# The first norm of a 17-stage transformer kernel: x turned by products with a diagonal of the roots, the gains applied in the copies out of PSUM

## The chip, the cores and the metric

The kernel runs on one core of one Trainium2 chip. The metric is the device time of one execution in microseconds; lower is better.

## The reference

Two transformer blocks follow one another on x of 256 tokens by 1024 channels, all in fp32. What matters here is the first thing that they do: a root-mean-square norm with gains, and the product with the first weight matrix.

```python
def rms_norm(x, g):          # x * rsqrt(mean(x*x) + eps) * g
...
def first_block(x, norm1_g, w_in, ...):
    for l in range(DEPTH):
        h = rms_norm(x, norm1_g[l])
        proj = h @ w_in[l]
        q, k, v, u = jnp.split(proj, [ATTN_WIDTH, 2 * ATTN_WIDTH, 3 * ATTN_WIDTH], axis=-1)
        ...   # attention over q, k, v; a gated causal convolution over u
        x = x + jnp.concatenate([attn, conv], axis=-1) @ w_out[l]
        h = rms_norm(x, norm2_g[l])
        x = x + (jax.nn.silu(h @ w_gate[l]) * (h @ w_up[l])) @ w_down[l]
    return x
```

Everything later (a feed-forward part, four more of them, two more mixers) is untouched by the change.

## The kernel before

Tokens lie in two tiles of 128 (t = 0, 1), channels in eight slices of 128 (k = 0 to 7, KT = 8). Weights come in units of 1 MB (`UNIT`): for the first mixer 1024 rows by 256 columns of `w_in`. Each fp32 operand is split in two fp32r parts, high and low. For weights ScalarE writes the high part `w_hi` (`split_hi`, L474) and VectorE the low one `w_lo` = raw - high (`split_lo`, L1892); for the turned activations the parts are `t_hi` and `t_lo`. A product is then three passes on TensorE: high by high, high by low, low by high. There are three raw buffers (`RAWS`) and six split slots. SyncE issues the loads in order, and the load of unit n waits for `lo_done` of unit n-3 (L424, L425): a raw buffer is free once VectorE has made the low part.

The engines' programs are written out by hand, one order for each engine, and tied by semaphores. The phases are an edge (norm and turning), a mixer, an edge, a feed-forward part and so on. The first edge, with `take == "input"`, goes so:

- SyncE loads the two tiles of x, then unit 0 in two halves (L435, L436), then units 1 and 2. ScalarE's queue loads the gains as one line (`g_line`, L954) and the identity (L955).
- TensorE spreads the gains over 128 partitions: two fp32 products of a column of ones with the line, 512 columns each, into banks 0 and 1 (L1315). `keep_running(3, 1)` (L1339) is one product of a constant with itself; its result is not used.
- ScalarE squares and sums the first half of each tile (`edge_stats`, L493) as soon as the tile is in, VectorE the other half (`mean_square`, L1987), and VectorE adds both and eps (L1990). GpSimd raises this to the power -0.5 (`inv_root`, L981): the root, one number for each token, one instruction for each tile. Behind these two, GpSimd's queue has six small setup loads (L986 to L991).
- VectorE makes `xn` = gains * root * x in four pieces (`normed`, L1995), TensorE turns each by transposes with the identity (L1323, four for each piece, sixteen in all), ScalarE and VectorE copy the turned pieces out of PSUM as `t_hi` (L551, L2018), VectorE subtracts for `t_lo` (`turned`, L2004). Between these lie the halves of unit 0's high part (L484, L489) and low part (L2023, L2034).
- Unit 0 (`by_channels_first`, L1147) is 48 passes of 256 columns in two halves of k; each half is high by high, high by low, then low weights by high. Unit 1 (`by_channels_second`, L1169 to L1174) runs 16 passes before it first waits for the low parts of its own weights; the units after it go by `three` (L1120 to L1122).

Behind unit 0, TensorE turns some parameters (`turn_params`, L1334), ScalarE copies them (L565, L566). Then the first mixer runs: VectorE, ScalarE and GpSimd share the 31 taps of the convolution (L2203 and L2206; L711 and L715; L1040 and L1043), and GpSimd builds diagonal matrices of taps for TensorE (L1055) once VectorE has done `setup` (L2563, L2571). TensorE's next products wait in its own order behind these.

Of the kernel before, what the change touches and what calls it, by code (L numbers as in the profile page):

```python
# [63 lines left out]
def build(nc, a, out, phases):  # L64
    stack = ExitStack()
    with stack:
# [43 lines left out]
        xn = wv(0, T, D)  # L110
        junk = wv(5120, 2, D)
# [130 lines left out]
        second_hi = sem("second_hi")  # L242
        line_in = sem("line_in")
        ones_set = sem("ones_set")
        g_spread = sem("g_spread")
# [88 lines left out]
        for ph in phases:  # L334
# [25 lines left out]
            n_lo += {"edge": 2 * T * (ph.get("g") is not None), "ffn": 0, "mix": 4}[ph["kind"]]  # L360
# [38 lines left out]
        index_bank = (4, 5, 2, 3)  # L399

# [57 lines left out]
        def _(act):  # L458
# [87 lines left out]
            def input_turned(t, half):  # L546

                nx(x_T)
                act.wait_ge(x_T, 2 * half + t + 1)
                src = bank[phases[0]["xb"][t] + half].rearrange("p (k s) -> p k s", k=4)  # L550
                nc.scalar.activation(t_hi[:, 4 * half:4 * half + 4, t * P:(t + 1) * P], src, ACT.Copy).then_inc(t_hi_ok, 1)  # L551

            def edge(ph):
                if ph["take"] == "input":
                    edge_stats(ph, 0)
                    edge_stats(ph, 1)
                    input_turned(0, 0)
                    first_half()
                    nx(x_T)
                    input_turned(0, 1)  # L560
                    input_turned(1, 1)
# [405 lines left out]
        def _(pool):  # L967
# [30 lines left out]
            def next_rows(post):  # L998

                if post and n_post < len(posts):  # L1000
                    pool.wait_ge(yg_done, 2 * T * n_post)
                    pool.dma_start(g_row[:, :], posts[n_post]["row"].partition_broadcast(P)).then_inc(grow_in, 16)
                if n_pre < len(pres):
                    pool.wait_ge(xn_ready, 2 * T * (n_pre + 1))
                    pool.dma_start(g_pre[:, :], pres[n_pre]["g"].partition_broadcast(P)).then_inc(gpre_in, 16)
# [105 lines left out]
        def _(pe):  # L1111
# [28 lines left out]
            def by_channels_first(b):  # L1140

                wh, wl = w_cols(0)
                def part(half, w, x, start=False, stop=False):

                    for c in range(2):
                        for k in range(4 * half, 4 * half + 4):
                            mm = nc.tensor.matmul(bank[b][:, c * S:(c + 1) * S], w[:, k, c * P:(c + 1) * P], x[:, k, :],  # L1147
                                                  start=start and k == 0 and c == 0, stop=stop and k == KT - 1 and c == 1)
                    return mm

                for half in range(2):
                    pe.wait_ge(hi_done if half else half_hi, 1)
                    pe.wait_ge(t_hi_ok, 2 * half + 1)
                    pe.wait_ge(second_hi, 1)
                    part(half, wh, t_hi, start=half == 0)
                    pe.wait_ge(t_lo_ok, 2 * half + 2)
                    part(half, wh, t_lo)
                    pe.wait_ge(lo_done if half else half_lo, 1)
                    mm = part(half, wl, t_hi, stop=half == 1)
# [17 lines left out]
            def tile_ready(t, k):  # L1177

                if k % 4 == 0:
# [128 lines left out]
            def edge(ph):  # L1308
                if ph["g"] is None:
                    return  # L1310
                if ph["take"] == "input":
                    pe.wait_ge(ones_set, 1)
                    pe.wait_ge(line_in, 16)
                    for h in range(2):
                        nc.tensor.matmul(bank[h][:, :], ones, g_line[:, h * 512:(h + 1) * 512], start=True, stop=True).then_inc(g_spread, 1)  # L1315
                    pe.wait_ge(consts_set, 2)
                    keep_running(3, 1)
                    pe.wait_ge(ident_in, 16)
                    for half in range(2):
                        for t in range(T):  # L1320
                            pe.wait_ge(xn_ready, nx(xn_ready))
                            for k in range(4 * half, 4 * half + 4):
                                mm = nc.tensor.transpose(bank[ph["xb"][t] + half][:, k % 4 * P:(k % 4 + 1) * P],  # L1323
                                                         xn[:, t, k * P:(k + 1) * P], ident[:, :])
                            mm.then_inc(x_T, 1)
# [541 lines left out]
        def _(dve):  # L1867
# [113 lines left out]
            def input_edge(ph):  # L1981
# [11 lines left out]
                def normed(t, h):  # L1993
                    hv = slice(h * 512, (h + 1) * 512)
                    nc.vector.scalar_tensor_tensor(out=xn[:, t, hv], in0=bank[h][:, :], scalar=st[:, 2 + t:3 + t],  # L1995
                                                   in1=x_sb[:, t, hv], op0=ALU.mult, op1=ALU.mult).then_inc(xn_ready, 1)

                def turned(t, half):
                    if (t, half) == (1, 0):
                        dve.wait_ge(second_hi, 1)  # L2000
                    else:
                        dve.wait_ge(t_hi_ok, (1, 2 + t)[half])
                    ks, ts = slice(4 * half, 4 * half + 4), slice(t * P, (t + 1) * P)
                    nc.vector.tensor_tensor(t_lo[:, ks, ts], bank[ph["xb"][t] + half].rearrange("p (k s) -> p k s", k=4),  # L2004
                                            t_hi[:, ks, ts].bitcast(F32), ALU.subtract).then_inc(t_lo_ok, 1)
# [3 lines left out]
                dve.wait_ge(g_spread, 1)  # L2009
                dve.wait_ge(rstd_ready, nx(rstd_ready))  # L2010
# [621 lines left out]
```

## Time and profile before

| | us |
|---|---|
| median of 3 runs | 1287.6 |
| lowest, highest | 1285.88, 1287.77 |
| the profiled execution, its own time | 1287.3 |
| its span, first to last instruction | 1285.4 |
| outside the span | 1.9 |
| TensorE busy in the span | 1274.2 (99%) |
| weight loads busy | 1088.2 (85%) |
| VectorE busy | 838.1 (65%) |
| ScalarE busy | 676.7 (53%) |
| GpSimd busy | 120.1 (9%) |

Busy means that an instruction of the engine was under way; matmuls overlap each other, so the steady pace of an engine is read from how far apart their starts are, not from their durations. Times of rows are microseconds from the first instruction. A "PEld" row is a weight load, which every matmul has. An fp32 product shows as two matmuls, a transpose or an fp32r product as one.

### The profile page before, as it was taken

What the parts mean: (1) busy time and instruction counts of PE and PEld (TensorE: products, weight loads), DVE (VectorE), ACT (ScalarE), POOL (GpSimd) and SP (SyncE); (2) the same over time, 40 slices, a digit from 0 to 9 for tenths busy, and PEclk for the clock granted to TensorE, in tenths of its full rate; (3) what the DMA queues carried; (4) which work ended last, traced back from release to release, by engine and by line L of the source; (5) the groups of instructions that cost most, each with busy time, mean ns of one, the idle gap of its engine ahead of it and who ended that gap; (6) DMA issues with size and microseconds to landing.
All of it is one profiled execution on the core that took longest, in us unless ns stands there. A gap on an engine that the chain in (4) does not pass through costs nothing.

```text
span 1285.4 us, 18283 instructions
## 1 busy us (share of the span) xinstructions
PE 1274.2 (99%) x7072; PEld 1088.2 (85%) x7072; DVE 838.1 (65%) x1102; ACT 676.7 (53%) x903; POOL 120.1 (9%) x135
## 2 busy tenths in 40 slices
PE   8999999999999999999999999999999999999998
PEld 7978888888888888887888888888888877888886
DVE  7997655565655548898765556655565776675552
ACT  5876554443544435656564444544454665564441
POOL 4970000000000000021000000000002120000000
PEclk9999999999999999999999999999999999999999
DMA  9525765563765543527565555575553755475540
GB/s 278 175 83 192 253 210 196 196 210 120 241 201 188 188 150 122 174 88 241 197 223 185 183 194 163 199 260 196 190 186 128 245 160 165 148 239 185 184 145 33
DMA packets 174350, 234.95 MB, mean 183 GB/s; under 512 B 4351, under 2 KB 154127, under 8 KB 174288
## 3 DMA queue, kind: packets, MB, share of 16 engines
q1 hardware_dynamic: 170368, 223.52, 52.9%
q0 software_dynamic: 3184, 9.37, 2.4%
q10 hardware_dynamic: 736, 1.19, 0.3%
q8 instruction: 43, 0.70, 0.2%
q14 instruction: 19, 0.16, 0.0%
HBM read 233.03 MB, written 1.05 MB: 182 GB/s over the span
## 4 chain that ended last, share of the span: by engine, by line
PE 90%; POOL 3%; DVE 3%; ACT 1%; DMA 1%; issue 1%; DVEq 0%; SPq 0%; POOLq 0%; ACTq 0%
PE psum L1225 23%; PE psum L1120 14%; PE psum L1121 14%; PE psum L1122 14%; PE psum L1233 12%; PE psum L1246 2%; POOL ws L1043 2%; PE psum L1188 2%; PE psum L1187 2%; PE psum L1186 2%; PE psum L1250 1%; PE psum L1457 1%; PE psum L1348 1%; POOL ws L1040 1%; PE psum L1505 1%
## 5 line engine op out<-in xcount | busy, mean ns | idle before, releaser
L1892 DVE TENSOR_TENSOR w_lo<-raw,w_hi 128x2048 fp32r<-128x2048 f32 (+1 forms) x200 | 457.7, 2294 | 85.2 <-ACT w_hi L474 83.8
L474 ACT ACTIVATE w_hi<-raw 128x2048 fp32r<-128x2048 f32 (+1 forms) x212 | 403.4, 1907 | 34.5 <-PE psum L1122 13.7
L1225 PE MATMUL psum<-t_both,w_hi 128*128 128x512 f32 x1280 | 304.7, 390 | 0.0
L1225 PEld LDWEIGHTS psum<-t_both,w_hi 128*128 128x128 f32 x1280 | 237.4, 188 | 47.4
L1120 PE MATMUL psum<-w_hi,f_hi 128*128 128x512 f32 x488 | 192.8, 395 | 0.0
L1122 PE MATMUL psum<-w_hi,f_lo 128*128 128x512 f32 x488 | 190.2, 390 | 0.0
L1121 PE MATMUL psum<-w_lo,f_hi 128*128 128x512 f32 x488 | 190.1, 389 | 0.0
L1120 PE MATMUL psum<-w_hi,t_both 128*128 128x512 f32 (+2 forms) x464 | 166.0, 358 | 0.2
L1122 PE MATMUL psum<-w_hi,t_both 128*128 128x512 f32 (+2 forms) x464 | 162.3, 350 | 0.0
L1121 PE MATMUL psum<-w_lo,t_both 128*128 128x512 f32 (+2 forms) x464 | 162.3, 350 | 0.0
L1233 PEld LDWEIGHTS psum<-t_both,w_lo 128*128 128x128 f32 x1280 | 158.9, 192 | 3.1
L1233 PE MATMUL psum<-t_both,w_lo 128*128 128x256 f32 x1280 | 159.8, 283 | 0.0
L589 ACT ACTIVATE ws<-psum 128x512 f32<-128x512 f32 x40 | 23.9, 597 | 256.1 <-PE psum L1233 256.1
L2064 DVE TENSOR_TENSOR ws<-psum,ws 128x512 f32<-128x512 f32 x40 | 27.6, 690 | 196.3 <-ACT ws L589 196.3
L981 POOL TENSOR_TENSOR st<-st,minus_half 128x1 f32<-128x1 f32 (+3 forms) x35 | 31.2, 891 | 1084.3 <-DVE st L1939 764.7
L1122 PEld LDWEIGHTS psum<-w_hi,f_lo 128*128 128x128 f32 x488 | 91.6, 188 | 19.3
L1120 PEld LDWEIGHTS psum<-w_hi,f_hi 128*128 128x128 f32 x488 | 91.6, 188 | 18.6 <-issue 0.5
L1121 PEld LDWEIGHTS psum<-w_lo,f_hi 128*128 128x128 f32 x488 | 91.7, 188 | 18.1
L1120 PEld LDWEIGHTS psum<-w_hi,t_both 128*128 128x128 f32 x464 | 87.7, 189 | 15.5 <-issue 3.7
L1122 PEld LDWEIGHTS psum<-w_hi,t_both 128*128 128x128 f32 x464 | 87.6, 189 | 11.7
L1121 PEld LDWEIGHTS psum<-w_lo,t_both 128*128 128x128 f32 x464 | 87.8, 189 | 10.3
L685 ACT ACTIVATE ws<-ws,st 128x128 f32<-128x128 f32 x80 | 35.4, 445 | 18.8 <-DVE st L2167 18.8
(218 smaller groups left out, 1291.1 us busy)
## 6 DMA issues: line engine op xcount, KB each, us to landing
raw<-in_ffn_wg SPq DMA_DIRECT2D x44, 1024.0 KB, 5.6
raw<-in_ffn_wu SPq DMA_DIRECT2D x44, 1024.0 KB, 5.4
raw<-in_ffn_wd SPq DMA_DIRECT2D x44, 1024.0 KB, 5.0
raw<-in_even_w_in SPq DMA_DIRECT2D x12, 1024.0 KB, 5.3
raw<-in_odd_w_in SPq DMA_DIRECT2D x12, 1024.0 KB, 5.3
raw<-in_w_gate SPq DMA_DIRECT2D x11, 1024.0 KB, 5.6
raw<-in_w_up SPq DMA_DIRECT2D x11, 1024.0 KB, 5.4
raw<-in_w_down SPq DMA_DIRECT2D x11, 1024.0 KB, 5.1
```

The lines of the kernel that those rows point to most:

```text
L474: nc.scalar.activation(w_hi[:, n % SLOTS, 0:w], raw[:, n % RAWS, 0:w], ACT.Copy).then_inc(hi_done, 1)
L685: nc.scalar.activation(p_buf[:, h % 2, lo:hi], s_buf[:, h % 2, lo:hi], ACT.Exp, scale=-1.0, bias=L["nmax"][:, c:c + 1], accum_out=L["sum"] ...
L981: nc.gpsimd.tensor_tensor(v, v, minus_half[:, 0:1].broadcast_to([P, v.shape[1]]), ALU.pow).then_inc(rstd_ready, 1)
L1043: nc.gpsimd.tensor_tensor(acc[:, 1::2, :], acc[:, 1::2, :], product[:, tap % 2, :, :], ALU.add)\
L1120: nc.tensor.matmul(o, lh, rh, start=start, stop=False)
L1121: nc.tensor.matmul(o, lh, rl, start=False, stop=False)
L1122: return nc.tensor.matmul(o, ll, rh, start=False, stop=stop)
L1186: nc.tensor.matmul(out, t_hi[:, k, ts], wh(k), start=k == 0, stop=False)
L1225: mm = nc.tensor.matmul(bank[b + c][:, :], wh[:, k, c * P:(c + 1) * P], t_both[:, k, :, :].rearrange("p a s -> p (a s)"), start=k == 0 and ...
L1233: mm = nc.tensor.matmul(bank[b + c][:, 0:S], wl[:, k, c * P:(c + 1) * P], t_hi[:, k, :], start=k == 0 and low_first, stop=k == KT - 1 and ...
L1892: nc.vector.tensor_tensor(w_lo[:, n % SLOTS, 0:w], raw[:, n % RAWS, 0:w], w_hi[:, n % SLOTS, 0:w].bitcast(F32), ALU.subtract).then_inc(lo_ ...
L2064: nc.vector.tensor_tensor(halves(f_s[:, b, :]), halves_of(4)[0], f_b[:, 0, :, :], ALU.add).then_inc(gate_sum, 1)
```

## The change

1. **TensorE first.** `keep_running(3, 28)` comes first, where it was `keep_running(3, 1)` behind the spread. The spread of the gains is gone. In its place eight products of a 1x128 piece of the line with one one put the gains as a column for each slice k into bank 2 (`gains_T` is raised behind the last).
2. **ScalarE first.** Its first compute instruction is now the copy of these eight columns to `gain_col`, which waits for `gains_T`. `edge_stats` for both tiles stands behind it. Then it writes `root_at_diag[0]`, the identity scaled by tile 0's roots; VectorE writes the one of tile 1.
3. **Turning.** `normed` and the transposes are gone. TensorE multiplies each 128x128 block of x, as weights, with the diagonal matrix of its tile: eight fp32 products for each tile, into `first_T(k)`, where slice k has both tiles side by side (256 columns).
4. **Copies.** `t_hi` for k = 0, 1 is made by VectorE, for 2 to 7 by ScalarE, one instruction of 256 columns for each k with the gain as its scale. `t_lo` is (PSUM * gain) - `t_hi` on VectorE, eight instructions of 256 columns.
5. **Orders.** Unit 0's passes go k by k: high weights by `t_hi` for k 0 to 3, low weights by `t_hi` for 0 to 3, high weights by `t_lo` for 0 to 3, then the same for 4 to 7. ScalarE makes the first half of `w_hi` before its `t_hi` and the second half behind them. Waits on counts are adapted (`tile_ready`, GpSimd's `next_rows`).

```diff
@@ ScalarE
             def edge(ph):
                 if ph["take"] == "input":
+                    act.wait_ge(gains_T, 1)
+                    nc.scalar.activation(gain_col, bank[2][:, 0:KT], ACT.Copy).then_inc(gains_kept, 1)
                     edge_stats(ph, 0)
                     edge_stats(ph, 1)
-                    input_turned(0, 0)
+                    act.wait_ge(ident_in, 16)
+                    act.wait_ge(rstd_ready, 1)
+                    nc.scalar.activation(root_at_diag[0], ident[:, :], ACT.Copy, scale=st[:, 2:3]).then_inc(root_diag, 1)
                     first_half()
-                    nx(x_T)
-                    input_turned(0, 1)
-                    input_turned(1, 1)
+                    act.wait_ge(gains_kept, 1)
+                    for k in range(2, KT):
+                        first_hi(k)
                     second_half()
@@ TensorE, edge
+                    pe.wait_ge(consts_set, 2)
+                    keep_running(3, 28)
                     pe.wait_ge(ones_set, 1)
                     pe.wait_ge(line_in, 16)
-                    for h in range(2):
-                        nc.tensor.matmul(bank[h][:, :], ones, g_line[:, h * 512:(h + 1) * 512], start=True, stop=True).then_inc(g_spread, 1)
-                    pe.wait_ge(consts_set, 2)
-                    keep_running(3, 1)
...
+                    for k in range(KT):
+                        mm = nc.tensor.matmul(bank[2][:, k:k + 1], g_line[:, k * P:(k + 1) * P], ones[:, 0:1], start=True, stop=True)
+                    mm.then_inc(gains_T, 1)
+                    for t in range(T):
+                        pe.wait_ge(root_diag, t + 1)
+                        for k in range(KT):
+                            nc.tensor.matmul(first_T(k)[:, t * P:(t + 1) * P], x_sb[:, t, k * P:(k + 1) * P], root_at_diag[t],
+                                             start=True, stop=True).then_inc(x_scaled, 1)
@@ TensorE, unit 0
+                pe.wait_ge(half_hi, 1)
+                for k in (0, 1):
+                    pe.wait_ge(dve_hi, k + 1)
+                    high(k, t_hi, start=k == 0)
+                for k in (2, 3):
+                    pe.wait_ge(act_hi, k - 1)
+                    high(k, t_hi)
+                pe.wait_ge(half_lo, 1)
+                low(0)
+                for k in range(4):
+                    pe.wait_ge(first_lo, k + 1)
+                    high(k, t_lo)
...
@@ VectorE, input_edge
                 mean_square(0)
                 mean_square(1)
-                dve.wait_ge(g_spread, 1)
-                dve.wait_ge(rstd_ready, nx(rstd_ready))
-                normed(0, 0)
...
+                dve.wait_ge(ident_in, 16)
+                dve.wait_ge(rstd_ready, nx(rstd_ready, 2))
+                dve.wait_ge(root_diag, 1)
+                nc.vector.tensor_scalar(root_at_diag[1], ident[:, :], st[:, 3:4], None, ALU.mult).then_inc(root_diag, 1)
+                dve.wait_ge(gains_kept, 1)
+                dve.wait_ge(x_scaled, KT + 2)
+                for k in range(2):
+                    nc.vector.tensor_scalar(t_hi[:, k, :], first_T(k), gain_col[:, k:k + 1], None, ALU.mult).then_inc(dve_hi, 1)
                 dve.wait_ge(half_hi, 1)
                 h = slice(0, UNIT // 2)
                 nc.vector.tensor_tensor(w_lo[:, 0, h], raw[:, 0, h], w_hi[:, 0, h].bitcast(F32), ALU.subtract).then_inc(half_lo, 1)
...
+                for k in range(4):
+                    low(k)
+                dve.wait_ge(half_lo, 1)
+                dve.wait_ge(hi_done, 1)
+                h = slice(UNIT // 2, UNIT)
+                nc.vector.tensor_tensor(w_lo[:, 0, h], raw[:, 0, h], w_hi[:, 0, h].bitcast(F32), ALU.subtract).then_inc(lo_done, 1)
+                for k in range(4, KT):
+                    low(k)
```

## Rows read from the trace of the kernel before

**Rows 1.** The page's busy shares; tenths in 40 slices.

```profile
PE 1274.2 (99%) x7072; PEld 1088.2 (85%) x7072; DVE 838.1 (65%) x1102; ACT 676.7 (53%) x903; POOL 120.1 (9%) x135
PE   8999999999999999999999999999999999999998
```

**Rows 2.** Waits of weight loads, 17 us to the end: total, times, longest.

```profile
PEld psum L1505 <- issue: 5.6, 15, 0.9
PEld psum L1457 <- issue: 5.3, 19, 0.4
...
PEld psum L1470 <- POOL ws L1012: 0.9, 2, 0.6
```

**Rows 3.** Timeline of TensorE to 19.5 us: start, us, what, count.

```profile
3.30 3.75 PE L1315 MATMUL psum<-ws 1*128 1x512 f32 x4 [3.30 <-DMA ws<-in_norm_g]
6.98 0.79 PE L1339 MATMUL psum<-mean_w 128*128 128x128 f32 x2
8.03 3.65 PE L1323 MATMUL psum<-ident,ws 128*128 128x128 f32 x16 [0.26 <-DVE ws L1995]
11.32 2.28 PE L1147 MATMUL psum<-t_both,w_hi 128*128 128x256 f32 x16
...
16.32 1.12 PE L1147 MATMUL psum<-t_both,w_lo 128*128 128x256 f32 x8
17.37 0.49 PE L1334 MATMUL psum<-ident,ws 20*128 20x20 f32 x2
```

**Rows 4.** Timeline, the other engines, 0.7 to 8 us.

```profile
0.78 0.21 POOL L975 MEMSET mean_w<- 128x128 f32 x1
4.65 0.63 ACT L493 ACTIVATE ws<-x_sb 128x512 f32<-128x512 f32 x1 [0.90 <-DMA x_sb<-in_x]
5.50 0.21 DVE L1990 TENSOR_SCALAR st<-st 128x1 f32<-128x1 f32 x1
5.86 0.55 POOL L981 TENSOR_TENSOR st<-st,minus_half 128x1 f32<-128x1 f32 x1 [4.87 <-DVE st L1990]
6.18 0.69 DVE L1987 CUSTOM_DVE_ANT_0 ws<-x_sb 128x512 f32<-128x512 f32 x1 [0.47 <-DMA x_sb<-in_x]
7.30 0.56 POOL L981 TENSOR_TENSOR st<-st,minus_half 128x1 f32<-128x1 f32 x1 [0.89 <-DVE st L1990]
```

**Rows 5.** Timeline, fp32 products later in the kernel, near 100 us.

```profile
99.25 1.86 PEld L1838 LDWEIGHTS psum<-mean_w,g_row 128*128 128x128 f32 x16 [0.64 <-ACT g_row L791]
102.53 0.61 PE L1844 MATMUL psum<-ident,st 128*128 128x128 f32 x4
```

**Rows 6.** Windows at the end: busy (count) by engine, PEclk, DMA, GB/s.

```profile
1270.00:1279.30 9.30, 9.30 (x43) 7.36 (x41) 2.82 (x5) 1.46 (x4) 0.56 (x1) 1.00 0.15 58
1279.40:1281.30 1.90, 0.00 (x0) 0.00 (x0) 1.12 (x4) 0.67 (x2) 0.55 (x1) 1.00 0.00 0
1281.40:1285.40 4.00, 0.00 (x0) 0.00 (x0) 1.04 (x2) 0.00 (x0) 0.00 (x0) 0.50 0.35 131
```

**Rows 7.** Timeline of ScalarE and VectorE, 10 to 18 us.

```profile
9.64 1.05 ACT L484 ACTIVATE w_hi<-raw 128x1024 fp32r<-128x1024 f32 x1
10.61 1.28 DVE L2004 TENSOR_TENSOR t_both<-psum,t_both 128x512 fp32r<-128x512 f32 x2
11.80 1.21 DVE L2023 TENSOR_TENSOR w_lo<-raw,w_hi 128x1024 fp32r<-128x1024 f32 x1
14.14 1.21 DVE L2034 TENSOR_TENSOR w_lo<-raw,w_hi 128x1024 fp32r<-128x1024 f32 x1
15.27 2.28 DVE L1892 TENSOR_TENSOR w_lo<-raw,w_hi 128x2048 fp32r<-128x2048 f32 x1
17.89 0.19 ACT L565 ACTIVATE p_col<-psum 128x20 f32<-128x20 f32 x1 [2.84 <-PE psum L1334]
17.98 0.27 ACT L566 ACTIVATE tap_col<-psum 128x124 f32<-128x124 f32 x1
```

**Rows 8.** Timeline, 256-column instructions out of PSUM, ScalarE and VectorE.

```profile
21.51 0.84 ACT L698 ACTIVATE ws<-psum,p_col 128x256 f32<-128x256 f32 x2
23.85 0.88 DVE L2220 SCALAR_TENSOR_TENSOR ws<-psum,p_col,ws 128x256 f32<-128x256 f32 x2 [0.99 <-PE psum L1174]
```

**Rows 9.** The chain that ended last, 17 to 30 us: start, us, what.

```profile
17.58 9.67 DMA raw<-in_w_in
27.27 1.92 ACT w_hi L474
29.66 2.70 POOL ws L1040
```

More of the change, by code:

```diff
@@ L241, in build @@
         half_lo = sem("half_lo")
[L242 removed]
+        gains_T = sem("gains_T")
+        gains_kept = sem("gains_kept")
+        root_diag = sem("root_diag")
+        x_scaled = sem("x_scaled")
+        dve_hi = sem("dve_hi")
+        act_hi = sem("act_hi")
+        first_lo = sem("first_lo")
         line_in = sem("line_in")
         ones_set = sem("ones_set")
[L245 removed]
         setup_in = [sem(f"setup_in{i}") for i in range(3)]
@@ L359, in build @@
                 n_x += 2 * T
-            n_lo += {"edge": 2 * T * (ph.get("g") is not None), "ffn": 0, "mix": 4}[ph["kind"]]
+            n_lo += {"edge": 2 * T * (ph.get("g") is not None and ph.get("take") != "input"), "ffn": 0, "mix": 4}[ph["kind"]]
             n_rstd += {"edge": T * (ph.get("take") == "post") + T * (ph.get("g") is not None), "ffn": 0,
@@ L1142, in by_channels_first, with high @@
                 wh, wl = w_cols(0)
-                def part(half, w, x, start=False, stop=False):
+                def high(k, x, start=False, stop=False):
                     for c in range(2):
-                        for k in range(4 * half, 4 * half + 4):
-                            mm = nc.tensor.matmul(bank[b][:, c * S:(c + 1) * S], w[:, k, c * P:(c + 1) * P], x[:, k, :],
-                                                  start=start and k == 0 and c == 0, stop=stop and k == KT - 1 and c == 1)
-                    return mm
@@ L1151, in by_channels_first @@
[L1151 to L1159, printed above, removed]
+                        mm = nc.tensor.matmul(bank[b][:, c * S:(c + 1) * S], wh[:, k, c * P:(c + 1) * P], x[:, k, :],
+                                              start=start and c == 0, stop=stop and c == 1)
@@ new lines, in high, with low @@
+                    return mm
+                def low(half):
+                    for k in range(4 * half, 4 * half + 4):
+                        for c in range(2):
+                            nc.tensor.matmul(bank[b][:, c * S:(c + 1) * S], wl[:, k, c * P:(c + 1) * P], t_hi[:, k, :], start=False, stop=False)
+                pe.wait_ge(half_hi, 1)
[5 more added lines that the diff above has]
+                    high(k, t_hi)
@@ new lines, in by_channels_first @@
+                pe.wait_ge(half_lo, 1)
[3 more added lines that the diff above has]
+                    high(k, t_lo)
+                pe.wait_ge(hi_done, 1)
+                for k in range(4, KT):
+                    pe.wait_ge(act_hi, k - 1)
+                    high(k, t_hi)
+                pe.wait_ge(lo_done, 1)
+                low(1)
+                for k in range(4, KT):
+                    pe.wait_ge(first_lo, k + 1)
+                    mm = high(k, t_lo, stop=k == KT - 1)
@@ L1177, in tile_ready @@
             def tile_ready(t, k):
-                if k % 4 == 0:
+                if k % 4 == 0 and fresh[0] is not None:
                     pe.wait_ge(t_lo_ok, fresh[0] + 2 * t + k // 4 + 1)
@@ L1991, in mean_square, with low @@
                                             ALU.add, ALU.add).then_inc(ms_ready, 1)
[L1993 to L2005, printed above, removed]
+                def low(k):
+                    if k >= 2:
+                        dve.wait_ge(act_hi, k // 2 * 2)
+                    nc.vector.scalar_tensor_tensor(out=t_lo[:, k, :], in0=first_T(k), scalar=gain_col[:, k:k + 1], in1=t_hi[:, k, :].bitcast(F32),
+                                                   op0=ALU.mult, op1=ALU.subtract).then_inc(first_lo, 1)
@@ L2030, in edge @@
                     input_edge(ph)
-                    dve.wait_ge(half_lo, 1)
-                    dve.wait_ge(hi_done, 1)
-                    h = slice(UNIT // 2, UNIT)
-                    nc.vector.tensor_tensor(w_lo[:, 0, h], raw[:, 0, h], w_hi[:, 0, h].bitcast(F32), ALU.subtract).then_inc(lo_done, 1)
                     cur[0] = 1
```

39 lines of the change are left out of this document (13 added, 26 removed).

## The prediction

> **What bounds the kernel now.** I read the page first. TensorE is busy for 99% of the span and in every one of the 40 slices [rows 1]. A busy share alone doesn't make it the bound, so I asked next what its weight loads waited for once unit 0 was over. From 17 us to the end the longest single wait is 0.9 us, and the largest group on another engine's work adds up to 0.9 us [rows 2]; the rest is the fixed half microsecond at the head of small groups. So from the first product of unit 0 on TensorE runs nearly without a gap, and whatever moves the end of unit 0 moves the end of the kernel by nearly the same. Next comes the timeline of the start, where the change lies: TensorE's first products start at 3.30, the sixteen transposes at 8.03, unit 0 at 11.32, and unit 0 ends at 17.4 [rows 3]. The question of this prediction is therefore one number: when does unit 0 end now?
>
> Two paces are to be seen there. The sixteen transposes fill 3.65 us, and the last one's own latency is 0.42 of it, so their starts are 0.213 us apart; sixteen passes of 256 columns behind them fill 2.28 us, about 0.12 to 0.13 apart [rows 3]. Later in the kernel four fp32 matmuls of 128 columns fill 0.61 us with 0.27 for one, and sixteen loads of one-column products fill 1.86 with 0.19 for one: 0.11 us apart in both [rows 5]. So the array is at 1.2 GHz until about 11.3 and at 2.4 GHz behind that. It rises after 3.3 to 3.6 us in which the transposes ran without a gap. It did not rise for the 3.75 us of one-row products before them. A fall shows too, at the end of the kernel: 1.9 us without products are still granted 1.00, the next 4 us 0.50 [rows 6].
>
> **The change part by part.** I build the new start forward, TensorE first.
>
> Step 1, `keep_running(3, 28)`. One product is two matmuls [rows 3], so 28 are 56. Their constant is set at 1.0 [rows 4] and nothing else is waited for, so they start at 1.1. At the low pace 0.213 they last 11.9 us, at the high one 0.11 they last 6.2: the end lies between 7.3 and 13.0. I take a rise at 4.7, after the same uninterrupted run as in the trace: 17 matmuls until then, 39 at 0.11 behind, the end at 9.0. These matmuls do nothing else, so in front of anything they hold back they cost their full time.
>
> Step 2, the gains. Eight fp32 products are 16 matmuls with a 128-column weight load each; by the one-column group 0.11 each [rows 5], 1.8 us (3.4 at the low pace). `gains_T` comes with 0.25 latency at about 11.1.
>
> Step 3, what waits for it. ScalarE's first instruction now waits for `gains_T`, and behind it stand both `edge_stats`. This is the place that decides. The copy is 0.2 us [rows 7], so the squares of tile 0 start at T0 = 11.3 instead of 4.65 [rows 4], although x has been there for 6.6 us. VectorE's sum, GpSimd's root and everything else wait behind it. From T0: the root of tile 0 is there at +1.8 (6.41 less 4.65), ScalarE's diagonal matrix (0.27, as the 124-column copy [rows 7]) at +2.1. VectorE can start the squares of tile 1 only at about +1.1; its part of them, sum, root (0.56) and the matrix give +3.1.
>
> Step 4, x times the diagonal. Sixteen fp32 products are 32 matmuls where sixteen transposes were 16. At 0.11 they last 3.5 us, at 0.213 6.8. They start at T0 + 2.1 = 13.4. TensorE has then had nothing at all for 2.5 us, and only one-row, one-column work for 1.8 us ahead of that; the trace shows a fall within about 2 us of the last product [rows 6], and that one-row work did not hold or lift the clock [rows 3]. So I take 1.2 GHz again at 13.4, and a rise after the same run as before, 3.6 us: 17 matmuls, then 15 at 0.11. The end is 13.4 + 3.6 + 1.65 = 18.6. Without the fall it is 16.9; without a rise 20.2.
>
> The Trainium skill (TensorE: Matmul & The Clock Gate, Part 4) says that transposes don't count as activity for the clock the way products do. The trace agrees that all sixteen ran at the low pace, but the first products behind them were fast at once, so here the measurement decides. Under the page's rule the rise in the old kernel would be put down to the products before the transposes, and my rise in step 1 could be later by as much as the bounds of that step hold.
>
> The same page (Part 3, the cost of the semaphore tail) prices each product that raises a semaphore at 26 ns, and `x_scaled` is raised by all sixteen. By it the sum would be 0.4 us larger. No row here isolates it.
>
> Step 5, unit 0. Its 48 passes at 0.12 are 5.8 us, unchanged. VectorE's share begins when slices 0 and 1 of tile 1 are in PSUM, 20 of the 32 matmuls in, at 17.5. It has two scalings, the half of `w_lo`, four low parts, the other half and four more: ten PSUM instructions of 256 columns at 0.33 (half of the 512-column pitch, 0.60 [rows 7]) to 0.44 [rows 8], two halves at 1.13: 5.6 to 6.7, and it ends at 23.1 to 24.2. ScalarE has six `t_hi` at about 0.38 [rows 8], the last one when the products are over, then the second half (1.05), by about 20. Its first half lies under the products. TensorE, from 18.6, ends at 24.4, with VectorE's last low parts just ahead of it. That is 7.0 us behind 17.4.
>
> What is removed and comes back: four `normed` (2.8 us on VectorE) and the transposes. They lay ahead of unit 0 and their removal is in the sum already, as the new chain doesn't hold them.
>
> Step 6, what is late next. VectorE's low part of unit 1 starts 7 to 8 us later, about 23.5, and takes 2.3 [rows 7]: TensorE can do unit 1's first 16 passes (1.9 us) from 24.9 meanwhile, so it doesn't stop. The loads of units 3 and 4 go out with `lo_done` of 0 and 1. In the old kernel the load of unit 4 took 9.67 us [rows 9] because it ran beside unit 3's load and the six loads of GpSimd's queue. Those loads are issued after the roots, now at about 14.2, with raw buffers full and nothing beside them, and are in before unit 3's load goes out; nearer 5 to 6 us for a load gives ScalarE's split of unit 4 about 4 us late, not 7. GpSimd's taps hang on that (29.66 [rows 9]) and are late by less than TensorE. So the convolution chain is no new bound; the few waits on other engines shrink, for which I give back 0.6 us.
>
> The unlisted edits (`tile_ready`, `next_rows`, ten small waits) cost nothing: TensorE's waits there are met by work that ended earlier, and GpSimd's first g_pre load already has its own place. Uncovered they'd be an instruction of some 0.05 us each.
>
> Sum: +7.0 - 0.6 = +6.4 us. The profiled execution took 1287.3 (span 1285.4 and 1.9 around it), 0.3 under the median of the three runs; 1287.3 + 6.4 = 1293.7, and with the 0.3, 1294.0.
>
> **Rivals.** (a) The clock doesn't fall in the gap: a gap of 2.5 us is hardly longer than the 1.9 that was still granted 1.00 [rows 6]. Then the products with the diagonals end at 16.9, unit 0 at 22.8, and the time is +4.8: 1292.4. Against it stand 1.8 us of nearly idle work on top.
> (b) The rise comes much later, or `keep_running` stays at the low pace. Each microsecond of delay of the rise in step 1 costs 0.5 us; for all 56 slow and slow gains the end of unit 0 goes from 24.4 to about 30, +11.5: 1299. For it speaks that the rise before came 4.3 us after the first full product at 6.98, or 8 us after the first of all [rows 3]; this last reading would give T0 = 13.5 and 1296.3.
> (c) The other side: faster. If the 56 matmuls and the gains were over when x is in, at 4.65, the statistics would be as early as before, the diagonal matrices there at 7.2 and 8.2, the products done by 10.8 and unit 0 by 16.6: 0.8 us less, 1286.8, which is no change by measure. For more, the low pace would have to be lifted too. It would decide if a matmul of `keep_running` took under 0.03 us ((4.4 - 1.1 - 1.8)/56); the fastest row has 0.11. It is as good as excluded by that place.
> (d) The delay is absorbed later. It would take a stretch in which TensorE waits for loads or for another engine by several microseconds; the waits [rows 2] don't have one, and all but the 0.6 given back would be a surprise. If half of it is lost the time is 1290.8; if all but 2 us, 1289.3.
>
> **How the numbers follow.** Forecast (fall, rise as before) 0.50, (a) 0.25, (b) 0.13, (c) 0.04, (d) 0.08. The predicted time is that of the first, 1294.0. Between 1290.2 and 1298 lie the forecast, (a), most of (b) and the milder (d): more than 8 in 10. A difference of 0.2% or 2.6 us is about what a measurement of this kernel can tell from no change. Slower than that: the first three and half of (d), 0.91; no change: half of (d) and most of (c), 0.07; faster 0.02.
>
> **What the new profile would show.** Step 1: 56 matmuls of `mean_w` from 1.1 to about 9, their starts 0.213 apart, then 0.11. Step 3: ScalarE's first squares at about 11.3, with TensorE as the releaser of the copy before them. Step 4: a gap of some 2.5 us on TensorE ahead of the products with `x_sb`, then 0.213 again. Step 5: unit 0's last pass at about 24.4. Step 6: from there on the two timelines run parallel, 6 to 7 us apart to the end. The prediction is wrong if the squares start before 9, if the pace of `keep_running` is below 0.11, or if the distance between the two kernels' TensorE shrinks by more than 1.5 us behind unit 0.

## The result, and the profile after

The changed kernel takes 1295.35 us (median of six runs, 1294.27 to 1296.02); the kernel before took 1286.8 in its six runs beside them (1285.88 to 1287.77). These medians are 8.55 us apart, or 0.66%; the ratio estimated from the runs is a little lower, 1.0057, with a 95% interval of 1.0048 to 1.0067. Either is well over the 0.2% that can be told from no change. Forecast were 1294.0, with 1290.2 to 1298.0. The profiled execution took 1295.7, its span is 1293.9 against 1285.4: +8.5, where the forecast had +6.4.

The time is lost in the first 26 us. TensorE's timeline of the start, which answers to [rows 3]:

```profile
1.04 8.61 PE L1370 MATMUL psum<-mean_w 128*128 128x128 f32 x56 [1.04 <-POOL mean_w L987]
9.58 1.94 PE L1347 MATMUL psum<-ws 1*128 1x1 f32 x16
14.24 6.15 PE L1352 MATMUL psum<-ws,x_sb 128*128 128x128 f32 x32 [2.71 <-ACT ws L569]
20.14 1.20 PE L1159 MATMUL psum<-t_both,w_hi 128*128 128x256 f32 x8
21.18 1.12 PE L1167 MATMUL psum<-t_both,w_lo 128*128 128x256 f32 x8
...
26.33 0.49 PE L1365 MATMUL psum<-ident,ws 20*128 20x20 f32 x2
```

`turn_params`, the first work behind unit 0, starts at 26.33, where it started at 17.37 [rows 3]. I use the start of this row as the mark for the end of unit 0 in every kernel below. Here it is 9.0 later than before. (The last experiment profiles the start of the old kernel a second time, and there the mark stood at 18.1. So differences of some tenths between marks mean little.) The order of events is the forecast's: 56 matmuls of a constant, 16 one-row matmuls for the gains, a gap of 2.71 in which TensorE waits for ScalarE's diagonal matrix (L569), and 32 matmuls with x.

What ScalarE and the other engines did meanwhile (their timelines, compare [rows 4]):

```profile
4.61 0.69 DVE L2018 CUSTOM_DVE_ANT_0 ws<-x_sb 128x512 f32<-128x512 f32 x1 [3.61 <-DMA x_sb<-in_x]
11.56 0.18 ACT L564 ACTIVATE ws<-psum 128x8 f32<-128x8 f32 x1 [7.80 <-PE psum L1347]
11.63 0.62 ACT L503 ACTIVATE ws<-x_sb 128x512 f32<-128x512 f32 x1
12.47 0.21 DVE L2021 TENSOR_SCALAR st<-st 128x1 f32<-128x1 f32 x1 [7.15 <-ACT ws L503]
12.83 1.38 POOL L993 TENSOR_TENSOR st<-st,minus_half 128x1 f32<-128x1 f32 x2 [11.84 <-DVE st L2021]
13.79 0.40 ACT L569 ACTIVATE ws<-ident,st 128x128 f32<-128x128 f32 x1 [0.83 <-POOL st L993]
18.98 0.88 DVE L2040 TENSOR_SCALAR t_both<-psum,ws 128x256 fp32r<-128x256 f32 x2 [4.38 <-PE psum L1352]
```

VectorE squares its half of tile 0 at 4.61, since x is there. ScalarE's half starts at 11.63, right behind the copy of the gains, and the copy had been waiting 7.80 us for TensorE. VectorE then waits 7.15 for that half, GpSimd 11.84. The chain that ended last runs through exactly these instructions, with no transfer in this part of it:

```profile
1.04 8.61 PE psum L1370 x56
9.65 1.89 PE psum L1347 x16
11.56 0.18 ACT ws L564
11.74 0.62 ACT ws L503 x2
12.47 0.22 DVE st L2021
12.83 0.86 POOL st L993
13.79 0.41 ACT ws L569
14.24 6.15 PE psum L1352 x32
```

The windows show the clock (busy and count by engine, then the granted clock, DMA share, GB/s):

```profile
5.50:12.20 6.70, 6.03 (x53) 5.82 (x52) 0.00 (x0) 0.64 (x3) 0.00 (x0) 1.00 1.10 350
12.30:19.10 6.80, 4.86 (x23) 4.86 (x24) 1.44 (x6) 2.00 (x5) 4.89 (x8) 0.50 0.73 182
19.20:25.00 5.80, 5.80 (x49) 5.60 (x48) 5.42 (x11) 5.04 (x8) 0.00 (x0) 1.00 0.13 47
```

It is at 1.00 (2.4 GHz) from 5.5, falls to 0.50 (1.2 GHz) at 12.3, in the gap behind the one-row matmuls, and stays there for the first 23 matmuls with x, whose starts are 0.213 apart; the nine behind them are at the high pace, 0.112 to 0.128 apart. Ahead of the first rise the profile has no record of the clock and a window reads 1.00 whatever the pace; there I go by how far apart the starts are.

### The profile page after: what moved, and what is told of

It is laid out like the page before. It is cut to its first block, busy times and chain, and to the rows that moved or that the text cites. A ratio compares the mean times of both kernels' runs of the same rounds, so it can differ in the third digit from the quotient of the medians.

```text
span 1293.9 us, 18450 instructions
## 1 busy us (share of the span) xinstructions
PE 1282.8 (99%) x7154; PEld 1099.4 (85%) x7154; DVE 836.3 (65%) x1104; ACT 677.0 (52%) x908; POOL 119.2 (9%) x135
## 4 chain that ended last, share of the span: by engine, by line
PE 96%; DVE 2%; ACT 1%; POOL 1%; issue 0%; DVEq 0%; ACTq 0%; POOLq 0%
PE psum L1255 23%; PE psum L1133 15%; PE psum L1134 15%; PE psum L1135 15%; PE psum L1263 12%; PE psum L1276 2%; PE psum L1218 2%; PE psum L1217 2%; PE psum L1216 2%; PE psum L1488 1%; PE psum L1280 1%; PE psum L1379 1%; PE psum L1536 1%; PE psum L1501 1%; PE psum L1370 1%; DVE w_lo L1923 1%
## 5 line engine op out<-in xcount | busy, mean ns | idle before, releaser
L1134 PEld LDWEIGHTS psum<-w_lo,f_hi 128*128 128x128 f32 x488 | 91.7, 188 | 18.1
```

The lines of the kernel that those rows point to most:

```text
L1134: nc.tensor.matmul(o, lh, rl, start=False, stop=False)
```

## The experiments

Theory: the change loses its time because ScalarE's statistics stand behind `gains_T`, and so behind `keep_running(3, 28)` and the gains; to this comes the low clock in the products with x. Rivals: the new way of turning x is itself the dearer one; or the constant products pay for themselves with the clock; or what is late in the first 26 us is made up for, or added to, later. For each run I give median and range, the ratio to the kernel before in the same job with its 95% interval, the mark of the profiled execution, and the span less the mark, which is all that comes behind unit 0 (1268.0 in the kernel before, 1267.6 in the changed one).

**Statistics first.** ScalarE's wait and copy are moved behind the statistics and the diagonal matrix; TensorE's program is untouched.

```diff
 if ph["take"] == "input":
-    act.wait_ge(gains_T, 1)
-    nc.scalar.activation(gain_col, bank[2][:, 0:KT], ACT.Copy).then_inc(gains_kept, 1)
     edge_stats(ph, 0)
     ...
     nc.scalar.activation(root_at_diag[0], ...).then_inc(root_diag, 1)
+    act.wait_ge(gains_T, 1)
+    nc.scalar.activation(gain_col, bank[2][:, 0:KT], ACT.Copy).then_inc(gains_kept, 1)
```

> The changed kernel with one edit: ScalarE's copy of the gain columns, and its wait for them, stand behind the squares of both tiles and the diagonal matrix of tile 0; TensorE still starts with 28 products. Theory A (the time is lost because the statistics wait for the gains, and these for the 28 products): the squares start at 4.65 again, the diagonal matrix of tile 0 is there at 7.3 and waits for TensorE, which goes from the gains (end 11.4) straight into the products with x, at the high pace (0.11): these end near 15.1, unit 0 near 21.2, 5 us ahead of the changed kernel: 1290.2 to 1290.8. Theory B (the doubled matmuls for x and the 256-column copies cost the time, whatever the order): within 1.5 us of the changed kernel's 1295.35.

Measured: 1291.67 (1291.41 to 1292.12), 1.0031 [1.0018, 1.0044], mark 21.90, behind it 1268.2. Its timeline:

```profile
6.65 0.39 ACT L567 ACTIVATE ws<-ident,st 128x128 f32<-128x128 f32 x1
...
1.04 9.27 PE L1370 MATMUL psum<-mean_w 128*128 128x128 f32 x56 [1.04 <-POOL mean_w L987]
10.24 1.94 PE L1347 MATMUL psum<-ws 1*128 1x1 f32 x16
12.11 3.84 PE L1352 MATMUL psum<-ws,x_sb 128*128 128x128 f32 x32
```

The diagonal matrix is there at 7.0 instead of 14.2, the gap on TensorE is gone, and with it the low clock: 3.84 for the products with x instead of 6.15. Unit 0 ends 4.4 earlier, 2.1 by the earlier start (although the constant's matmuls took 0.66 longer in this profile) and 2.3 by the clock. Of the 9.0 us 4.5 are left: the constant's matmuls and the gains' hold up x now, where they held up ScalarE. It came 1 us above what was expected: about 0.7 at the mark, from the constant's matmuls, and 0.6 behind unit 0 (below).

**The number of constant products.** One instead of 28, and 56, all else as in the change.

```diff
-    keep_running(3, 28)
+    keep_running(3, 1)      # the other run: keep_running(3, 56)
```

> The changed kernel with keep_running(3, 1) in place of 28. Theory A: the gains' line comes at 3.3, the gains take 16 matmuls at the low pace (3.4 us), so ScalarE starts its squares at 6.9 and not 11.6; the products with x start at 9.5, all or nearly all of them at the low pace (6.2 to 6.8 us), unit 0 ends near 22: 1291.0, 4.3 us less than the changed kernel. A rival (the 28 products are worth their time because without them the clock stays low for longer): the low pace reaches into unit 0, whose 48 passes then take up to 6 us more, and the time is 1295 or above.

> The changed kernel with keep_running(3, 56). Theory A: 56 more matmuls at 0.112 hold back the gains, the statistics and all behind them by 6.25 us one to one, give or take the phase in which the clock rises in the products with x: 1300.2 to 1302. Theory B (the 28 products lie beside the loading of x and the weights): under 1 us more, 1296.3 at most.

Measured: with one, 1289.66 (1289.10 to 1290.67), 1.0017 [1.0008, 1.0026], mark 20.13, behind it 1267.2. With 56, 1302.13 (1301.8 to 1302.33), 1.0112 [1.0097, 1.0128], mark 32.96, behind it 1267.1. TensorE with one:

```profile
2.31 3.54 PE L1347 MATMUL psum<-ws 1*128 1x1 f32 x16 [0.47 <-DMA ws<-in_norm_g]
8.56 5.62 PE L1352 MATMUL psum<-ws,x_sb 128*128 128x128 f32 x32 [2.72 <-ACT ws L569]
20.13 0.49 PE L1365 MATMUL psum<-ident,ws 20*128 20x20 f32 x2
```

and with 56:

```profile
1.04 15.01 PE L1370 MATMUL psum<-mean_w 128*128 128x128 f32 x112 [1.04 <-POOL mean_w L987]
20.64 6.50 PE L1352 MATMUL psum<-ws,x_sb 128*128 128x128 f32 x32 [2.71 <-ACT ws L569]
```

From 28 to 56 the span grows by 6.2, 56 times 0.112: each constant matmul stands on the path at its full time. (The mark moves by 6.6: two more of the products with x are at the low pace.) From 28 to one the span falls by 6.6. What the 27 products buy is a faster pace for the gains, 1.94 us instead of 3.54, and nothing for x, which begins at the low pace in every one of the three. So the rival that they pay for themselves is out. With one product the time is 1.3 us lower than expected, since the gains' line comes 1 us earlier than I had it and the low pace lasts for fewer of the products with x; with 56 it lies 0.1 above the range. The gap of 2.7 is the same in all three kernels: it is the length of the chain from `gains_T` to the diagonal matrix.

**The gap filled.** Twelve more constant products behind the gains, while TensorE waits for the diagonal matrix anyway.

```diff
     mm.then_inc(gains_T, 1)
+    keep_running(3, 12)
```

> The changed kernel with 12 more products of the constant behind the gains, where TensorE stood idle from 11.5 to 14.2 (24 matmuls at 0.112, 2.7 us). If the fall of the clock costs what the sum says: no fall at 12.3, the 32 matmuls with x 0.112 apart from the first on, 3.6 us instead of 5.9, and VectorE gets its first slices at 16.7 instead of 19.0: 2.3 us less, 1293.0. If the clock falls all the same (the one-row products count for nothing), or if VectorE's chain sets the end of unit 0 anyway, less than 0.5 us is gained.

Measured: 1293.82 (1293.61 to 1294.26), 1.0048 [1.0035, 1.0062], mark 23.30, behind it 1268.5. Timeline and windows:

```profile
8.86 1.94 PE L1347 MATMUL psum<-ws 1*128 1x1 f32 x16
10.73 2.94 PE L1371 MATMUL psum<-mean_w 128*128 128x128 f32 x24
13.52 3.84 PE L1353 MATMUL psum<-ws,x_sb 128*128 128x128 f32 x32
```

```profile
4.00:17.00 13.00, 13.00 (x115) 12.83 (x115) 2.89 (x10) 3.18 (x9) 4.88 (x8) 1.00 0.97 307
```

The clock holds. The mark is 3.03 earlier than in the changed kernel: 2.31 by x at the high pace, 0.72 because the rise came earlier in this profile (at 3.9). So the low clock by itself costs 2.3 us of the 9.0, as expected. In the medians only 1.5 us is to be seen: in the profile of this kernel 0.9 us more passes behind unit 0, where the clock falls once near 106 us (below).

**Statistics first, and fewer constant products.** Both edits together, with 17 and with one.

> The order of the first experiment (statistics ahead of the gains' copy) with keep_running(3, 17). In all five kernels so far the span is 1267.1 to 1268.4 us plus the end of unit 0. TensorE is through with the 34 matmuls near 7 and with the gains near 9, 2 us behind the diagonal matrix of tile 0 (7.3); the products with x run at the high pace to 12.5, unit 0 ends near 18.7. Theory A: 1287.9 to 1288.9, 1.2 us over the kernel before and 3 under the order alone. If it is 1290 or more, something else than TensorE's work ahead of x counts.

> The same order with keep_running(3, 1). The gains end at 5.9, the squares start at 4.6, the diagonal matrix is there at 7.3 and TensorE waits for it. The products with x start at 7.3 at the low pace; where the clock rises decides: at best 11.5 (20 slow matmuls, the rest 1.3 us), end 12.9, unit 0 near 19.1; at worst all 32 slow, end 14.1, unit 0 near 20.3. 1288.1 to 1289.5. Against the kernel before it shows what the new way of turning x costs by itself when neither the 28 products nor the order of ScalarE hold it up: 1.5 to 3 us. If the new way is better by itself, it is under 1287.

Measured: with 17, 1288.40 (1287.33 to 1290.17), 1.0009 [1.0000, 1.0018], mark 20.74, behind it 1267.5. With one, 1288.12 (1287.72 to 1288.83), 1.0006 [0.9997, 1.0015], mark 18.20, behind it 1268.7. With one the time lies at the lower end of its range and can't be told from the kernel before. The cost of the new way by itself, which I had put at 1.5 to 3 us, comes out at 0.3 in the medians and 0.8 at the mark. With 17 the median is in the range, but the mark is 2 us late, and the eleven runs lie in two groups, 1287.33 to 1288.40 and 1289.96 to 1290.17. The profiled execution is of the slower group (1290.01). Its timeline and two windows show why it is late:

```profile
7.46 1.94 PE L1347 MATMUL psum<-ws 1*128 1x1 f32 x16
9.33 5.47 PE L1352 MATMUL psum<-ws,x_sb 128*128 128x128 f32 x32
```

```profile
6.20:9.50 3.30, 3.30 (x29) 3.16 (x29) 1.00 (x4) 1.94 (x5) 0.60 (x2) 1.00 1.11 344
9.60:12.90 3.30, 3.30 (x17) 3.30 (x17) 0.00 (x0) 0.01 (x1) 2.88 (x5) 0.50 1.10 348
```

There is no gap, and still the clock falls, in the products with x just behind the one-row ones. With 28 products and the same order (the first experiment) the same sixteen one-row products, without a gap as well, were followed by x at the high pace. So to close the gap is enough in some executions and not in others. That the faster group of this kernel is the one without the fall fits the 2 us between the groups, but no execution of it was profiled.

**Gains loaded as columns.** What is left of the change when no product is spent on the gains at all: a transfer brings them in as columns, and 18 constant products lie where TensorE waits for the roots anyway.

```diff
-act.dma_start(g_line, phases[0]["g"].unsqueeze(0)).then_inc(line_in, 16)
+act.dma_start(gain_col, phases[0]["g"].rearrange("(k p) -> p k", p=P)).then_inc(line_in, 16)   # behind the identity's load
...
-keep_running(3, 28)
-... (eight products into bank[2], gains_T, the copy to gain_col)
+keep_running(3, 18)
```

> The best that I see in the new way: the gains come as columns by a load of their own (1024 pieces of 4 bytes, behind the identity's load in the same queue) instead of 16 matmuls and a copy, and keep_running(3, 18) ends near 7.1, when the diagonal matrix is ready. Products with x from 7.3 to 10.9 at the high pace, VectorE's first slices at 9.7, unit 0 near 16.9: 0.5 us ahead of the kernel before, 1286.9 to 1287.5 against its 1287.8. If the small pieces arrive later than 9.7, or delay x and the weights, it is slower than before by as much.

Measured: 1287.18 (1286.24 to 1287.98), 0.9997 [0.9988, 1.0006], mark 17.13, behind it 1268.9.

```profile
1.04 5.88 PE L1363 MATMUL psum<-mean_w 128*128 128x128 f32 x36 [1.04 <-POOL mean_w L985]
7.36 3.84 PE L1345 MATMUL psum<-ws,x_sb 128*128 128x128 f32 x32 [0.44 <-ACT ws L567]
17.13 0.49 PE L1358 MATMUL psum<-ident,ws 20*128 20x20 f32 x2
```

The mark is 0.24 before that of the old kernel. The old start alone was 0.7 apart in its two profiles, so this is no gain. Turning x by products with a diagonal, with the gains in the copies, comes to the same time as `normed` and transposes, once nothing stands ahead of the statistics, the gains cost TensorE nothing and the clock is up when x comes. Against this kernel the changed one is 9.20 late at the mark, and its 9.20 are 6.88 by which the products with x start late (14.24 less 7.36) and 2.31 by which they last longer.

**The old kernel with the clock lifted early.** Ten constant products ahead of the spread of the gains, three behind it.

> The kernel before with keep_running(3, 10) ahead of the spread of the gains and (3, 3) behind it in place of (3, 1), nothing else. If the clock rises by 6 or so and stays, the sixteen transposes are 0.11 apart instead of 0.213, but VectorE hands over its four pieces at 7.9, 8.6, 9.3 and 10.0, so they end at 10.5 instead of 11.3, and unit 0 starts when VectorE's copy of tile 1 is done (10.7): 0.5 us gained, unit 0 ends at 16.9, no difference that the time can show. Rival: the spread comes later (7.1 instead of 7.0 at best; later still at the low pace), VectorE's first piece with it, and nothing is gained.

Measured: 1287.47 (1286.07 to 1289.24), 0.9998 [0.9989, 1.0007], mark 17.25, behind it 1268.9. A miss in its mechanism: the mark should have come at 16.9.

```profile
5.16 1.98 PE L1317 MATMUL psum<-ws 1*128 1x512 f32 x4
7.98 3.60 PE L1325 MATMUL psum<-ident,ws 128*128 128x128 f32 x16
```

```profile
4.70:8.00 3.30, 3.30 (x16) 1.79 (x14) 2.58 (x8) 1.38 (x4) 1.10 (x2) 1.00 1.07 365
8.10:11.40 3.30, 3.30 (x17) 3.28 (x17) 3.29 (x6) 2.14 (x3) 1.23 (x2) 0.50 1.11 342
```

The one-row spread ran at 1.00. Behind it came the six matmuls of the constant, still at the high pace, and at 8.0, as the transposes began, the clock fell.

**The other order of passes.** The kernel with loaded columns, but unit 0's passes as before the change (in each half, low weights last).

> The kernel with the gains loaded as columns, and in unit 0 the old order of passes in each half: low parts of x before low parts of the weights. VectorE makes t_lo one slice in 0.39 us, TensorE uses one in 0.24, so in this order it waits for t_lo where it did the low weights before. Worked out from the trace of the kernel with the loaded columns: unit 0 ends at 17.7 instead of 17.05, 0.65 us later, which is what the new order of passes is worth here; in the time it is hardly to be told. If the end is at 17.1 or less, the new order is worth nothing.

Measured: 1287.22 (1286.82 to 1288.94), 0.9999 [0.9990, 1.0008], mark 18.05, behind it 1269.1. The mark is 0.92 later than in the kernel with the new order: TensorE waits for VectorE's low parts of x ahead of L1157. So the new order is worth 0.7 to 0.9 us to the new way of turning (0.65 expected), less than can be told in the median.

```profile
11.03 1.19 PE L1157 MATMUL psum<-t_both,w_hi 128*128 128x256 f32 x8
12.50 1.68 PE L1157 MATMUL psum<-t_both,w_hi 128*128 128x256 f32 x8 [0.28 <-DVE t_both L2023]
```

**What comes behind unit 0.** Span less mark is 1267.1 to 1268.0 in some kernels and 1268.2 to 1269.1 in the others. In the second kind, and only there, the clock is at 0.50 for a stretch between 100 and 110 us, behind a stretch of short waits and one-column products for a variance. This happens in some executions of a kernel and not in others. Of the kernel with the old order of passes, six runs took 1286.82 to 1287.22 with a mean granted clock of 0.999 or 1.000, and five 1288.46 to 1288.94 with 0.997 or 0.998; the profiled one is of the five and has the fall. The profile of the kernel with loaded columns is of this kind too:

```profile
98.05 1.95 PE L1862 MATMUL psum<-mean_w,g_row 128*128 128x1 f32 x16 [0.20 <-ACT g_row L801]
...
96.00:100.00 4.00, 3.81 (x26) 3.12 (x25) 3.15 (x3) 3.97 (x5) 0.00 (x0) 1.00 0.00 0
100.00:103.40 3.40, 3.40 (x11) 2.82 (x12) 0.16 (x1) 1.31 (x1) 1.27 (x2) 0.50 0.88 270
```

To see whether these products are the cause, I let them move 128 columns of the constant instead of one, in the kernel with loaded columns and in the old one.

```diff
-mm = nc.tensor.matmul(bank[4][:, S + t:S + t + 1], V["sq"][:, ct, t * P:(t + 1) * P], mean_w[:, 0:1], ...
+mm = nc.tensor.matmul(bank[4][:, S + t * P:S + (t + 1) * P], V["sq"][:, ct, t * P:(t + 1) * P], mean_w[:, :], ...
-nc.vector.tensor_scalar(st[:, 10:12], bank[4][:, S:S + T], ...
+nc.vector.tensor_scalar(st[:, 10:12], bank[4][:, S:2 * S:P], ...
```

> The kernel with the gains loaded as columns, plus one edit near 98 us: the sixteen matmuls of the variance move 128 columns of the constant instead of one (they were 0.11 apart with one column and should stay so with 128), so that the waits and one-column products there are no longer one quiet stretch. In the profile without this edit unit 0 ended 0.4 us ahead of the kernel before, but the granted clock fell to 0.50 from 100 to 103.4, in four other kernels of this study too, and the span was 0.6 us longer. If that fall is the cause: granted clock 1.00 from 100 to 110, the span 1267.1 to 1267.8 plus the end of unit 0, 1284.3 to 1284.9, and a median 0.5 to 1.3 us under the kernel before. If the fall costs nothing, the median is as without the edit, 0.3 to 0.6 under.

> The kernel before with the wide variance alone. Where the clock falls near 100 depends on when the clock's grants change in that execution, so some executions of the kernel before should have the fall and some not. If it costs 1 to 1.5 us where it comes, the median falls by 0.3 to 1 us and the slowest executions go. If nothing moves (under 0.2 us), the fall is not worth anything in the kernel before.

Measured: with loaded columns 1286.55 (1286.27 to 1286.82), 0.9992 [0.9983, 1.0001], mark 17.31, behind it 1267.2. The old kernel so widened: 1286.96 (1285.88 to 1287.37), 0.9994 [0.9985, 1.0003], mark 18.09, behind it 1267.1. The first one's rows:

```profile
98.23 2.05 PE L1862 MATMUL psum<-mean_w,g_row 128*128 128x128 f32 x16 [0.20 <-ACT g_row L801]
...
100.00:103.40 3.40, 3.40 (x20) 2.87 (x19) 1.40 (x4) 2.02 (x3) 1.27 (x2) 1.00 0.83 256
```

In neither profile is there a fall, behind unit 0 the first one is 1.7 us shorter than without the edit, and 128 columns cost 0.1 us more than one for all sixteen. Two profiles without a fall could be chance, as five of the eleven with the narrow products have none either. The times say more: all eleven runs of the old kernel so widened are at 1287.37 or less, with a granted clock of 0.999 or 1.000, while 23 of the 27 of the old kernel beside them are above that. The median is 0.9 lower, as expected, though the interval of the ratio takes in no change. With loaded columns the median is the lowest of the study, 1.3 us under the 1287.89 of the kernel before in that job, and 8.8 under the change; but its interval still reaches 1.0001, so against the kernel before nothing more than no change is shown.

## Why the prediction was right, and where it was off

**The bound** (unit 0's end moves the kernel's end): right. (The waits at the head of small groups, read as a fixed half microsecond, are 0.28 and 0.37 us on average in [rows 2].) Over all thirteen profiles the mark lies between 17.1 and 33.0 and what is behind it between 1267.1 and 1269.1; most of the 2 us there goes with the clock near 100 us, none of it with the mark.

**Step 1**, the constant: forecast to end at 9.0, ended at 9.6. The rise came at 5.5 instead of 4.7, and in two other profiles of the same 56 matmuls at 3.9 and 6.8. I had called 4.7 a choice between bounds, and this term is one that varies from run to run by 1.4 us at the matmuls' end.

**Step 2**, the gains: 16 matmuls, 1.94 us (1.8 forecast).

**Step 3**, the wait of ScalarE: this is the cause, as forecast. T0 was 11.63 for 11.3. The step from T0 to the diagonal matrix was sized too small, 2.6 for 2.1: the root took 0.86 instead of 0.55 and the matrix 0.40 instead of 0.27, for which I had used the row of a copy of 124 columns out of PSUM.

**Step 4**, the products with x: the fall was right and rival (a), no fall, is out. The term that was mis-sized is the time at 1.2 GHz: I put 17 of the 32 matmuls at the low pace and it was 23, so unit 0 started 5.9 behind the first of them where 5.2 were forecast. In this kernel the fall hangs on the gap: filled with products, it left the clock at 1.00 although the one-row products stood ahead of it. That one-row work doesn't hold the clock, which I had taken from [rows 3], isn't in those rows; they only show that it didn't lift it.

**Step 5**, unit 0: 5.8 forecast, 6.2 measured from its first start to the mark. It had been 6.05 in the old kernel, so 5.8 was too low from the outset. VectorE's parts came just ahead as worked out: no new bound. With steps 1 to 4 this makes the mark 9.0 late instead of 7.0.

**Step 6**, 0.6 given back: 0.5, but this is luck. By 90 us the distance between the two kernels has shrunk from 9.0 to 8.0, some of it in waits of TensorE for ScalarE that are shorter than in the profile of the old kernel; 0.4 of it is lost again later. That is within the 1.5 us which I had named as the sign of being wrong. The same waits are as short in the old kernel with early constants, whose mark isn't late at all. The first of these three rows is from the kernel before, the second from the changed one, the third from the old one with early constants:

```profile
88.23 0.87 PE L1505 MATMUL psum<-ws 128*64 128x256 f32 x8 [0.57 <-ACT ws L667]
96.23 0.87 PE L1536 MATMUL psum<-ws 128*64 128x256 f32 x8 [0.35 <-ACT ws L679]
87.26 0.87 PE L1507 MATMUL psum<-ws 128*64 128x256 f32 x8 [0.36 <-ACT ws L667]
```

They start 70.9, 69.9 and 70.0 us behind the mark. So the shrinking doesn't come from unit 0 being late, and why the one profile of the old kernel has it longer is open. Rival (d), a delay absorbed later, is out.

**Rival (b)**, a later rise, held in its mild form; all 56 slow didn't happen. **Rival (c)** asked what is left when nothing holds the statistics back and put it at no change, 1286.8; the kernel with loaded columns comes nearest to that case and measures 1287.18 beside 1287.81. (Two prices of rivals don't add up as written: all 56 slow is +12.0 and not +11.5, and a delay absorbed but for 2 us is 1289.6. No chance hangs on it.)

In all, the forecast of the difference was about 2 us too low, all of the misses to one side: 0.8 in steps 1 to 3, 0.7 in step 4, 0.4 in step 5, 0.1 in step 6. The time itself was only 1.35 off, because the kernel before took 1286.8 beside the changed one and not the 1287.6 that the forecast started from. That is luck too. Most of the misses are a duration or a clock stretch taken from the old kernel for a place that had another history.

On the Trainium skill (TensorE: Matmul & The Clock Gate, Part 4), by which transposes don't count as activity: in the old kernel with early constants the clock fell at 8.0, then came sixteen transposes and nothing else, and it rose at 11.4, as the first product behind them ran, so this measurement still speaks against the page. But the rise isn't sure to come by then. The widened old kernel has the same start, and nine passes of unit 0 were still 0.214 apart behind the transposes (rise at 13.4), so that the first sixteen took 3.15 us instead of 2.28:

```profile
11.18 3.15 PE L1147 MATMUL psum<-t_both,w_hi 128*128 128x256 f32 x16
```

The semaphore tail (the Trainium skill, same page, Part 3) is given there as 26 ns for each increment behind a group of small products packed into the array, which these aren't. In the starts nothing of it is seen: x's products raise a semaphore sixteen times and their matmuls start 0.112 apart, as the constant's do, which raise none.

## What to carry to other kernels

When work is put at the head of one engine's program, look who waits for its last instruction, and what stands behind that wait on the waiting engine: here a 0.2 us copy of eight columns, needed only 7 us later, stood ahead of all of ScalarE's share of the statistics. Products that only keep the clock up are free as far as TensorE would wait anyway, and cost their full time beyond. Don't count products of one row among those that keep the clock up: here they didn't lift it, and with no gap behind them it stayed up in some kernels and fell in others.

## What the runs showed of the hardware that I had not expected

- Products of one row did not lift the clock. With one constant product, 16 of them in 3.54 us stayed at about 0.2 us apart, and x behind them began at 1.2 GHz. With the clock at 1.00, it fell 0.2 us behind 1.9 us of them (17 constant products) and 0.9 us behind 2.0 us of them (old kernel, early constants), though TensorE had no gap; with 28 constant products ahead and no gap it didn't fall. What decides isn't shown.
- An fp32 product costs nearly the same for one moved column and for 128: sixteen matmuls took 1.95 and 2.05 us. With the one-column products so widened no fall came behind them in two profiles, and no run of these two kernels had a granted clock under 0.999.
- The same one-column products brought the fall near 100 us in six of the profiles and not in the others (before and after among these), with no edit near there. What decides is open; the fall costs about 1.2 us by the means of the two kinds, and 1.7 us by the two groups of runs of the kernel with the old order of passes.
- GpSimd's first root took 0.55 us where the statistics ran as soon as x was in, and 0.86 in the four kernels where they waited for `gains_T`, while the second took 0.55 in the same profiles. In those four VectorE starts the squares of tile 1 before the root and not during it, as it does otherwise. Whether this is the reason wasn't tried.
